# Sparse attention's keys and first queries transposed between the tiles of the last projection, into the attention's own PSUM banks

## What is computed

```python
def c_layer(u, w_in, b_gate, pe_k, pe_v, wk1, wk2, wv1, wv2, w_out, cos, sin):
    q, kc, vc, ks, vs, kw, vw, gl = split_cols(u @ w_in, C_WIDTHS)
    q = partial_rope_2(q.reshape(b, s, C_HEADS, HEAD_DIM), cos, sin)
    ...
    o = nsa_mixer(q, kc, kv(vc), ks, kv(vs), kw, kv(vw), gl + b_gate, pe_k, pe_v, wk1, wk2, wv1, wv2)
    return o @ w_out

# nsa_mixer, per block of 128 tokens:
s_c = einsum('bqghd,bngd->bghqn', qb, kc) * scale        # 31 compressed keys
s_s = einsum('bqghd,bgqkd->bghqk', qb, k_g) * scale      # selected blocks
s_w = einsum('bqghd,bkgd->bghqk', qb, kw) * scale        # window
out = gb[..., 0:1] * o_c + gb[..., 1:2] * o_s + gb[..., 2:3] * o_w
```

## Time and profile before

| what | value |
|---|---|
| time, median of 3 runs | 2038.35 us (2037.58 to 2039.99) |
| the profiled execution's own time | 2038.36 us |
| its span, first to last instruction | 2036.5 us |
| PE busy | 1885.3 us (93%) |
| DVE, ACT, POOL busy | 1000.3 us, 814.8 us, 568.4 us |
| mean granted clock of the tensor engine | 0.973 |

### The profile page before, as it was taken

The page is one execution under the profiler, slowest core; times in us unless marked ns, Lnnn a source line. Parts: engine busy times, 40 slices in busy tenths (PEclk is TensorE's granted clock), DMA queues, the critical chain, the costliest instruction groups (busy, mean ns, idle before and its releaser), DMA issues.

```text
span 2036.5 us, 27987 instructions
## 1 busy us (share of the span) xinstructions
PE 1885.3 (93%) x10942; PEld 1469.3 (72%) x10942; DVE 1000.3 (49%) x1998; ACT 814.8 (40%) x1506; POOL 568.4 (28%) x403
## 2 busy tenths in 40 slices
PE   7999999998785999988999999999799999999997
PEld 6878889732222893457888888888767797888886
DVE  2161352511112425863366676822566714676777
ACT  5123642211112413364455544342266725445442
POOL 2344431011101220144421123233056533113211
PEclk9999999998998999999999999999899999999999
DMA  6223103799998330201123223411500012223321
GB/s 232 83 89 118 42 1 145 299 393 420 420 421 306 104 112 0 83 1 43 42 86 121 83 84 124 146 44 42 125 2 1 2 42 83 84 83 124 124 83 42
DMA packets 82324, 248.48 MB, mean 122 GB/s; under 512 B 12259, under 2 KB 15523, under 8 KB 69904
## 3 DMA queue, kind: packets, MB, share of 16 engines
q1 hardware_dynamic: 75936, 231.54, 30.8%
q0 software_dynamic: 4880, 9.89, 1.4%
q10 hardware_dynamic: 1376, 5.25, 0.6%
HBM read 241.89 MB, written 12.58 MB: 125 GB/s over the span
## 4 chain that ended last, share of the span: by engine, by line
PE 48%; DVE 4%; issue 2%; ACT 2%; POOL 0%; DVEq 0%; ACTq 0%
PE psA L1434 33%; PE psO L1592 2%; PE psT L1592 2%; PE psS L1592 2%; PE psO L1993 2%; PE psT L2030 1%; DVE x L2582 1%; PE psS L2021 1%; PE psA L1543 1%; PE psO L1494 1%; PE psT L1526 1%; PE psA L2021 1%; ACT big L2063 1%; DVE scr L3419 1%; PE psA L1303 1%
## 5 line engine op out<-in xcount | busy, mean ns | idle before, releaser
L1143 POOL TENSOR_TENSOR w_slot<-ring,w_slot 128x1024 fp32r<-128x1024 f32 (+2 forms) x80 | 208.6, 2621 | 542.2 <-ACT w_slot L2063 542.0
L1434 PE MATMUL psA<-hT_hi,w_slot 128*128 128x512 f32 x992 | 307.8, 389 | 0.0
L2063 ACT ACTIVATE w_slot<-ring 128x1024 fp32r<-128x1024 f32 (+2 forms) x178 | 191.9, 1088 | 176.9 <-PE psA L1434 77.0
L1434 PEld LDWEIGHTS psA<-hT_hi,w_slot 128*128 128x128 f32 x992 | 186.2, 188 | 38.6
L1434 PE MATMUL psA<-hT_lo,w_slot 128*128 128x512 f32 x496 | 192.9, 389 | 0.0
L2582 DVE TENSOR_TENSOR x<-psA,x 128x512 f32<-128x512 f32 (+1 forms) x204 | 121.1, 622 | 146.2 <-PE psA L1434 142.4
L2582 DVE TENSOR_TENSOR w_slot<-ring,w_slot 128x1024 fp32r<-128x1024 f32 x98 | 119.8, 1224 | 116.1 <-ACT w_slot L2063 116.1
L2063 ACT ACTIVATE big<-psA 128x512 f32<-128x512 f32 (+6 forms) x149 | 66.2, 469 | 270.6 <-PE psA L1434 139.8
L1434 PE MATMUL psA<-w_slot,hid_part 128*128 128x512 f32 x672 | 161.4, 389 | 0.0
L2063 ACT ACTIVATE scr<-scr,stat 128x384 f32<-128x384 f32 (+3 forms) x224 | 124.4, 556 | 70.7 <-DVE stat L3419 39.0
L1434 PEld LDWEIGHTS psA<-w_slot,hid_part 128*128 128x128 f32 x672 | 126.1, 188 | 26.2
(11 more groups left out here) (402 smaller groups left out, 4430.2 us busy)
## 6 DMA issues: line engine op xcount, KB each, us to landing
ring<-in_mlp_w SPq DMA_DIRECT2D x32, 2048.0 KB, 8.3
ring<-in_w_in SPq DMA_DIRECT2D x8, 2048.0 KB, 8.0
ring<-in_w_gate_e SPq DMA_DIRECT2D x14, 1024.0 KB, 16.9
ring<-in_w_up_e SPq DMA_DIRECT2D x14, 1024.0 KB, 21.1
ring<-in_w_down_e SPq DMA_DIRECT2D x13, 1024.0 KB, 27.1
big<-in_w_down_e SPq DMA_DIRECT2D x12, 1024.0 KB, 26.5
ring<-in_ab_w_in SPq DMA_DIRECT2D x5, 2048.0 KB, 7.8
scr<-in_w_down_e SPq DMA_DIRECT2D x7, 1024.0 KB, 25.0
```

Of the source, the lines that this page charges most:

```text
L1143: nc.gpsimd.tensor_tensor(part(w_lo, c), raw_piece(c), part(w_hi, c).bitcast(F32), ALU.subtract)\
L1434: ins = pe.matmul(o, a, b, start=(at == 1), stop=(at == 3 * len(terms)))
L2063: return nc.scalar.activation(o, i, f, **kw)
```

## The change

Keys and queries 0 to 3 leave the chain of jobs through `psA`. Keys 0 and 1 are turned behind tile 0 of the last projection piece, into `psS`; keys 2 and 3 behind tile 1, into `psT`; queries 0 and 1 (into `psO`) and 2 and 3 (into `psT`) behind tile 2 (`beside_queries`, called through `behind`). New semaphores count them (`nsa_turned` for PE's part, `query_lo` for DVE's), and the scores wait for them as they need them. Queries 4 to 7 and the four compressed products alternate in the attention's steps 4, 5, 6, 7, 8, 9, 12 and 13 (`NSA_STEPS`), still through `psA`; ACT takes each one step later, DVE a query two steps later. DVE's reading of the compressed values and the rotary embedding of the last query piece move into its step 2. `MORE_BANKS` goes from 12 to 16. The homes in SBUF follow: `nsa_q[0]` now lies where `hT_lo` lies, the left operand of the projection, so ACT writes no query before the last tile is done; `nsa_k` lies on two weight slots, and the weight pieces before change slots for it, with the same waits. POOL's and SP's lists keep their order.

```diff
-AHEAD, MORE_BANKS, PRESPLIT = 2, 12, (82, 86, 90, 94)
+AHEAD, MORE_BANKS, PRESPLIT = 2, 16, (82, 86, 90, 94)
...
-               ("turn_nk", 4), ("turn_nq", 8), ("cmps", 4), ("no", 3 * NT), ("tail5", NT + KD), ("mlp1", MLP_JOBS)):
+               ("nsa", 8), ("no", 3 * NT), ("tail5", NT + KD), ("mlp1", MLP_JOBS)):
...
+NSA_JOBS = (("query", 4), ("query", 5), ("cmp", 0), ("cmp", 1), ("query", 6), ("query", 7), ("cmp", 2), ("cmp", 3))
+NSA_STEPS = (4, 5, 6, 7, 8, 9, 12, 13)
...
-        a4_parts = (("keys", 4096), ("probs", 1024), ("cmp_scores", 2048), ("more_probs", 1024), ("queries", 4096), ("kv", NT * 776),
+        a4_parts = (("queries", 4096), ("probs", 1024), ("cmp_scores", 2048), ("more_probs", 1024), ("keys", 4096), ("kv", NT * 776),
...
+        def key_bank(c):
+
+            return (psS + psT)[c]
+
+        def early_bank(j):
+
+            return (psO + psT)[j]
...
-                at = (len(MLP_PIECES) - 4 + 2 * ((c - SPLIT_AT["nk"]) % 2) + (parts is w_lo)) % 4
-                return w_slots[0][at][:, 0:k * (c1 - c0)].rearrange("p (k n) -> p k n", k=k)
+                n, low = c - SPLIT_AT["nk"], parts is w_lo
+                at = w_slot[((2, 1), (3, 0), (2, 1), (0, 0), (3, 2), (1, 0), (3, 2), (1, 0))[n][low]]
+                first_word = 1024 if n == 3 and low else 0
+                return at[:, first_word:first_word + k * (c1 - c0)].rearrange("p (k n) -> p k n", k=k)
...
-            split_token_major("nq", "nq1", 2 * NT, low, halves=(1,))
+
+            def keys(c):
+
+                for t in range(NT):
+                    for half in range(2):
+                        ins = pe.matmul(key_bank(c)[HD * half:HD * (half + 1), t * P:(t + 1) * P],
+                                        kv2[:, t, 256 + HD * c:256 + HD * (c + 1)], ident, start=True, stop=True)
+                ins.then_inc(nsa_turned, 1)
+
+            def early_query(j):
+
+                for t in range(NT):
+                    ins = pe.transpose(early_bank(j)[:, t * P:(t + 1) * P], tok[:, t, j * P:(j + 1) * P], ident)
+                ins.then_inc(nsa_turned, 1)
+
+            def beside_queries(t):
+
+                if t < 2:
+                    keys(2 * t)
+                    keys(2 * t + 1)
+                elif t == 2:
+                    pe.wait_ge(heads_ready, 5)
+                    early_query(0)
+                    early_query(1)
+                    pe.wait_ge(query_lo, 10)
+                    early_query(2)
+                    early_query(3)
+
+            pe.wait_ge(sum_taken, KEPT_SUMS)
+            split_token_major("nq", "nq1", 2 * NT, low, halves=(1,), behind=beside_queries)
...
-                turn_twice(JOBS["turn_nk"] + c, [kv2[:, t, 256 + HD * c:256 + HD * (c + 1)] for t in range(NT)])
-            pe.wait_ge(heads_ready, 6)
-
-            def queries(j):
-
-                turn(JOBS["turn_nq"] + j, [tok[:, t, j * P:(j + 1) * P] for t in range(NT)])
+
+            def late_query(j):
+
+                if j == 4:
+                    pe.wait_ge(heads_ready, 6)
+                turn(nsa_job("query", j), [tok[:, t, j * P:(j + 1) * P] for t in range(NT)])
...
-                o = begin(JOBS["cmps"] + n)
+                if n == 0:
+                    copied_all(pe, "cmpc", 2)
+                    pe.wait_ge(query_lo, 14)
+                elif n >= 2:
+                    for j in (2 * n, 2 * n + 1):
+                        copied(pe, nsa_job("query", j))
+                o = begin(nsa_job("cmp", n))
...
-                    if i < 3:
-                        queries(i + 5)
-                    elif 6 <= i <= 9:
-                        if i == 6:
-                            copied_all(pe, "turn_nq", 8)
-                            copied_all(pe, "cmpc", 2)
-                        compressed_scores(i - 6)
+                    if i in NSA_STEPS:
+                        what, n = NSA_JOBS[NSA_STEPS.index(i)]
+                        if what == "query":
+                            late_query(n)
+                        else:
+                            compressed_scores(n)
                     if i < n_nsa:
                         it = nsa[i]
+                        if i in (0, 4, 8, 12):
+                            pe.wait_ge(query_lo, 10 + i // 4 + 1)
...
-            evac(JOBS["cmpc"], kc, 64)
             for c in range(4):
-                n = JOBS["turn_nk"] + c
-                product(act, n)
-                A(nsa_k[:, c // 2, c % 2, 0, :], bank(n)[:, :], ACT.Copy).then_inc(stack_hi, 1)
+                act.wait_ge(nsa_turned, c + 1)
+                A(nsa_k[:, c // 2, c % 2, 0, :], key_bank(c)[:, :], ACT.Copy).then_inc(stack_hi, 1)
 
             def queries(j):
 
-                n = JOBS["turn_nq"] + j
-                product(act, n)
-                A(query(j, 0)[0:HD, :], bank(n)[0:HD, :], ACT.Copy)
-                A(query(j, 1)[HD:P, :], bank(n)[HD:P, :], ACT.Copy).then_inc(stack_hi, 1)
+                if j < 4:
+                    act.wait_ge(nsa_turned, 4 + j + 1)
+                    o = early_bank(j)
+                else:
+                    product(act, nsa_job("query", j))
+                    o = bank(nsa_job("query", j))
+                A(query(j, 0)[0:HD, :], o[0:HD, :], ACT.Copy)
+                A(query(j, 1)[HD:P, :], o[HD:P, :], ACT.Copy).then_inc(stack_hi, 1)
...
-                    if i < 4:
-                        queries(i + 4)
-                    elif 6 <= i <= 9:
-                        n = JOBS["cmps"] + i - 6
-                        product(act, n)
-                        A(cmp_scores[:, i - 6, :], bank(n)[:, :], ACT.Copy).then_inc(proj_evacuated[n % 2], 1)
+                    if i in (1, 2):
+                        queries(i + 1)
+                    elif i - 1 in NSA_STEPS:
+                        what, n = NSA_JOBS[NSA_STEPS.index(i - 1)]
+                        if what == "query":
+                            queries(n)
+                        else:
+                            evac(nsa_job("cmp", n), cmp_scores[:, n, :])
...
-            for j in range(4):
+            product(act, job("nq", 4 * NT - 1))
+            for j in range(2):
                 queries(j)
+            evac(JOBS["cmpc"], kc, 64)
...
-            query_part(3)
-            n = JOBS["cmpc"] + 1
-            o = evac_to(n)
-            for q in range(4):
-                last = nc.vector.tensor_copy(vcBD[32 * q:32 * q + 32, HD * q:HD * q + HD],
-                                             o[32 * q:32 * q + 32, HD * (q % 2):HD * (q % 2) + HD])
-            last.then_inc(proj_evacuated[n % 2], 1)
-            query_rope((3,))
-
-            for c in range(4):
-                n = JOBS["turn_nk"] + c
-                dve.wait_ge(stack_hi, 6 + c + 1)
-                tt(nsa_k[:, c // 2, c % 2, 1, :], bank(n)[:, :], nsa_k[:, c // 2, c % 2, 0, :].bitcast(F32), ALU.subtract)\
-                    .then_inc(proj_evacuated[n % 2], 1)
+            for t in range(NT):
+                query_part(3, (t,))
+                for c in (2 * t, 2 * t + 1) if t < 2 else ():
+                    dve.wait_ge(stack_hi, 6 + c + 1)
+                    tt(nsa_k[:, c // 2, c % 2, 1, :], key_bank(c)[:, :], nsa_k[:, c // 2, c % 2, 0, :].bitcast(F32), ALU.subtract)\
+                        .then_inc(query_lo, 1)
+
+            def compressed_values():
+
+                n = JOBS["cmpc"] + 1
+                o = evac_to(n)
+                for q in range(4):
+                    last = nc.vector.tensor_copy(vcBD[32 * q:32 * q + 32, HD * q:HD * q + HD],
+                                                 o[32 * q:32 * q + 32, HD * (q % 2):HD * (q % 2) + HD])
+                last.then_inc(proj_evacuated[n % 2], 1)
...
-                    if 1 <= i <= 4:
-                        queries(i + 3)
+                    if i in (1, 3, 5):
+                        queries((i + 1) // 2)
+                    elif i == 2:
+                        compressed_values()
+                        query_rope((3,), a4["cmp_scores"])
+                    elif i - 2 in NSA_STEPS and NSA_JOBS[NSA_STEPS.index(i - 2)][0] == "query":
+                        queries(NSA_JOBS[NSA_STEPS.index(i - 2)][1])
```

More of the change, by code:

```diff
@@ L146, with nsa_job @@
                ("nk", 2 * NT), ("nv", 2 * NT), ("nqa", NT), ("cmpa", 5), ("nqb", 2 * NT), ("cmpb", 2), ("nqc", NT), ("cmpc", 2),
-               ("turn_nk", 4), ("turn_nq", 8), ("cmps", 4), ("no", 3 * NT), ("tail5", NT + KD), ("mlp1", MLP_JOBS)):
+               ("nsa", 8), ("no", 3 * NT), ("tail5", NT + KD), ("mlp1", MLP_JOBS)):
     JOBS[_n], WIDTH[_n] = _at, _w
     _at += _w
+NSA_JOBS = (("query", 4), ("query", 5), ("cmp", 0), ("cmp", 1), ("query", 6), ("query", 7), ("cmp", 2), ("cmp", 3))
+NSA_STEPS = (4, 5, 6, 7, 8, 9, 12, 13)
+def nsa_job(what, n):
+    return JOBS["nsa"] + NSA_JOBS.index((what, n))
 TAIL = {"wo": 1, "ao": 3, "mlp0": 4, "no": 5}
@@ L423, in build @@
         w_slots = [[w_slot[i] for i in at] for at in ((0, 2, 1, 3), (2, 3, 0, 1))]
```

(43 more changed lines are left out.)

11 lines of the change are left out of this document (7 added, 4 removed).

## The result

The changed kernel takes 2043.14 us (median of 20 runs, 2039.24 to 2048.55), the kernel before 2039.89 us (20 runs, 2035.52 to 2041.14): ratio 1.002, 95% interval 1.0014 to 1.0026. It is slightly slower, by about the 0.2% that I called no change, and the interval reaches beyond that. The profiled execution took 2044.48 us. The page begins (span; busy time, share and instructions by engine, cf.

What follows compares the result with a forecast made beforehand. The stretch was bound by a ring of short waits, no engine full. Legs of 25.1 us put score 17 3.2 us later; with 0.4 absorbed, 2038.35 + 2.8 = 2041.1 us, range 2033.8 to 2044.2.

Steps and rivals of the forecast that it cites:

- the forecast's own range: Whole run if the clock is back by 1489 us: 2039.8 to 2042.4 us, chance 0.48.
- Turns between the tiles: Four key and four query turns on a full PE delay the last projection tile by 5.6 us, at most 6.5.
- Last tile to first score: Query 0's high part on ACT, low part on DVE and hand-overs: 2.7 us instead of 16.3.
- Steps 0 to 6: First score to first compressed product, paced by DVE's list and query 4's bank: product at 1468.35 us, 8.6 us earlier.
- The legs: Six parts of steps 6 to 17, where late queries and compressed products hold each other up in psA: 25.1 us.
- Score 17: First score of 256 columns, from which PE is nearly full: starts at 1493.5 us, 3.2 us later than before.
- 0.4 us absorbed: PE's idle time in the 10 us behind the first 256-column score takes up 0.4 us, leaving +2.8 us.
- The clock: PE's granted clock falls to 0.50 near 1462 us and comes back at 1488.6 to 1491.0 us.
- slower, by the clock: Rival: pauses keep PE at the lower clock through step 17 and on; +4.1 to +6 us, 2043.5 us, chance 0.22.
- The rival in which the clock does not fall: Clock stays up or is back before step 6, so products and steps run faster: -1.9, 2036.5 us, chance 0.16.
- The rival in which the gain stays: ACT and DVE take queries 5 to 7 at once; first 256-column score 4 to 8 us earlier, 2032 us, chance 0.14.
- One mark of my own that would have said "wrong": First 256-column score before 1489 or after 1495 us, or another time from the attention there to the output projection.

Runs made afterwards that it cites:

- the repeat: The changed kernel, with no further edit, run and profiled once more; ratio to the kernel before 1.0007 to 1.0025.
- own banks: Changed kernel with queries 4 to 7 turned into the values' banks (psO) instead of psA; ratio to the kernel before 0.9998.
- the fill: Changed kernel with unread identity transposes on PE ahead of the waits of steps 0 to 13; ratio to the kernel before 0.9988 to 1.0006.
- the fastest: Changed kernel with late queries in psO, all turns behind the last tile and identity transposes only in PE's waits; 2033.18 us, 0.997 of the kernel before.

## Why the prediction was right, step by step

It said 2041.1 us, +2.8 on the profiled time of before. The medians lie 3.25 us apart, the profiled measures 3.8 us, and 6.9 in the repeat. The time itself, 2043.14 us, is above the forecast's own range (to 2042.4 us): the kernel before had a median of 2039.89 us in 20 runs, 1.5 more than in the 3 that I started from. So the difference bears the forecast out, and the absolute number does less so.

- *Turns between the tiles, +5.6 us.* 5.90 at the last tile. Right, inside the 6.5 of its upper end.
- *Last tile to first score 2.7 us.* 2.67. Right. What I did not work out is that the same banks, used behind the tile, would do it 1.6 us sooner.
- *Steps 0 to 6, DVE's list and query 4's bank.* 10.72 us for the 10.35 I had (1458.0 to 1468.35). Right, down to the reciprocal of 0.16 us (an estimate then; there are two of them). The bank's share is shown by the own banks, with which it takes 8.97 us.
- *The legs.* Predicted 4.3, 4.2, 3.4, 5.1, 2.7, 5.4, measured 4.37, 4.02, 3.39, 5.02, 2.71, 6.01: 25.5 for 25.1 us, and 13.3 before. This is where the gain went. The own banks give 4.35 us of it back, and 1.75 ahead of P0; the other 7.9 us beyond before's 13.3 stay with them, so the shared banks are shown for a part of it only. The sum charges the rest to the late queries' parts and the masks on DVE and ACT; no run takes that apart.
- *Score 17 +3.2 us.* +4.24: 0.27 more at the first score, 0.37 in steps 0 to 6, 0.4 in the legs (0.6 in the sixth, less in others; `MORE_BANKS` was not run by itself). 0.4 us absorbed: 0.46 (147.15 for 147.61); in the repeat, with the second fall of the clock, that stretch took 1.68 us more instead.
- *The clock.* Down from near 1462 to between 1488.6 and 1491.0: in before's time 1459.0 to 1489.7 in the first profile, 1491.8 and a second fall in the repeat. The return lies in the 1488.6 to 1491.0 us that I gave, the first time; since it moves between executions, that is partly luck. The forecast had no second fall. That is the term that I left out, and it makes the rival "slower, by the clock" true in the repeat, at +6.9 us, beyond its upper end of 6.
- *The rival in which the clock does not fall* was priced at -1.9 us. With the fill, score 17 comes 0.5 us earlier than before, 1.2 without the fill's own price (an estimate): the sign is right there, the size a little large; the measure, with its dip behind the fill, is 0.2 us longer.
- *The rival in which the gain stays* did not come about in the change. The Trainium skill (Perfetto Trace Analysis, "Matmuls") wants independent groups of matmuls in different PSUM banks. The runs agree in direction: banks also for the late queries gave 4.8 us back in the measure, and 8.0 us with the turns behind the tile. They don't agree with the 8 us below before that I priced by that rule: with own banks the measure is 1.0 us below before's, with the turns behind as well 4.2 us.

One mark of my own that would have said "wrong" was touched in the repeat: score 17 at 1495.5 us in before's time, and another time from there on (149.29 us for 147.61), both by the clock.

## What to carry to other kernels

Work that is brought forward pays only as far as the last thing that waits for it: here 8 us gained at the first product were spent again behind it, and banks for the four later queries, which had kept the old two, gave 6.1 us back. Give every tile of such a chain its own bank before moving any of it, and put a turn into a stretch where its engine waits; where PE is full, it only pushes the tile that everything hangs on. And compare two versions of a stretch in which the clock falls by marks ahead of its return, or with the clock kept up in both, since its return can move the end by as much as the edit.

## What the runs showed of the hardware

The granted clock of one program came back at different places in two executions, and in one it fell once more after some 3 us at 1.00, in 2.5 of which PE was busy for 1.22 us; 6 us of unbroken work at 0.50 followed before it was back. With transposes of the identity, 0.1 us each, ahead of PE's waits it stayed at 1.00 from the first score to score 17 in the kernel before (20.8 us); without them it was at 0.50 over the first part of that stretch, first score to P0, in which PE was busy 5.32 us of 10.97. In three other filled kernels it fell some microseconds behind the end of the fill (near 1477, 1481 and 1491 us), and in the fastest it fell near 1465 us in spite of it. Why it fell a second time in some executions and not in others stays open.
